# Second block: attention outputs with tokens on partitions, head norms on eight columns, no division of probabilities

## What is computed

```
p = jax.nn.softmax(s, axis=-1)                      # heads 0 to 7
oa, ob = moba_attention(...), dsa_attention(...)    # p @ v per head
z = einsum(q, k) * scale                            # heads 8 to 15
a = exp(log_sigmoid(z) + reverse_cumsum(log_sigmoid(-z), strictly after))
oc = a @ v
o = concatenate([oa, ob, oc])                       # (tokens, 16 heads, 64)
o = o * rsqrt(mean(o * o, over the 64) + 1e-6) * out_g
x = x + g2 * (o @ w_out)
```

## Time and profile before

| | |
|---|---|
| median of 3 runs | 2840.96 us |
| the profiled execution | 2840.38 us, of which its span is 2838.3 us |
| mean granted TensorE clock | 0.994 |
| PE, DVE, ACT, POOL busy | 98%, 70%, 48%, 8% |
| attention passes, layer 0 of the second block | from about 2008.6 us to 2063.2 us of the span |
| the same, second layer | from about 2566 us to 2621 us of the span |

### The profile page before, as it was taken

One profiled execution on the slowest core, in us unless ns is written; L12 is line 12 of the kernel. 1 busy time (PEld: TensorE's weight loads), 2 busy tenths in 40 slices (PEclk: granted clock), 3 DMA queues, 4 the chain that ended last, 5 costly groups with the idle time before them and its releaser, 6 DMA issues.

```text
span 2838.3 us, 37704 instructions
## 1 busy us (share of the span) xinstructions
PE 2773.7 (98%) x16040; PEld 2423.6 (85%) x16040; DVE 1974.6 (70%) x2225; ACT 1370.5 (48%) x1554; POOL 228.9 (8%) x201
## 2 busy tenths in 40 slices
PE   7999999999999999999999999999999999999999
PEld 6889999998888889999998887878878878787787
DVE  6768876655666678877655667677976676778644
ACT  5444545455444445545454444444644444446433
POOL 0000420000000000520000000003000000030000
PEclk9999999999999999999999999999999999999999
DMA  8655433445776655333446666653266666442453
GB/s 304 258 220 183 151 122 137 165 164 211 260 262 246 251 207 188 139 135 133 171 165 229 256 256 245 258 217 134 90 229 253 252 264 259 182 149 95 177 188 149
DMA packets 82039, 564.43 MB, mean 199 GB/s; under 512 B 9072, under 2 KB 10576, under 8 KB 15952
## 3 DMA queue, kind: packets, MB, share of 16 engines
q1 hardware_dynamic: 66272, 465.47, 44.9%
q0 software_dynamic: 15600, 96.55, 9.1%
HBM read 560.86 MB, written 1.12 MB: 198 GB/s over the span
## 4 chain that ended last, share of the span: by engine, by line
PE 82%; DVE 11%; ACT 3%; POOL 2%; DMA 1%; issue 1%; SPq 0%; POOLq 0%; ACTq 0%; DVEq 0%
PE ps L332 74%; DVE ring_lo L327 3%; ACT w_hi L320 1%; POOL qk L2038 1%; PE ps L899 1%; POOL rope_a L2034 1%; DVE a_hg L1806 1%; DMA rows<-mod_rows 1%; DVE e L1786 1%; DVE e L1785 1%; PE ps L1287 1%; DVE h_lo L576 0%; PE ps L1416 0%; PE ps L1442 0%; DVE e L993 0%
## 5 line engine op out<-in xcount | busy, mean ns | idle before, releaser
L327 DVE TENSOR_TENSOR ring_lo<-ring,w_hi 128x2048 fp32r<-128x2048 f32 x422 | 973.8, 2310 | 478.9 <-ACT w_hi L320 467.3
L320 ACT ACTIVATE w_hi<-ring 128x2048 fp32r<-128x2048 f32 x422 | 806.4, 1911 | 321.5 <-PE ps L332 197.9
L332 PE MATMUL ps<-w_hi,h_hi 128*128 128x512 f32 (+1 forms) x1920 | 729.1, 380 | 18.0 <-DVE ring_lo L327 9.3
L332 PE MATMUL ps<-w_hi,h_lo 128*128 128x512 f32 (+1 forms) x1920 | 716.4, 373 | 0.0
L332 PE MATMUL ps<-ring_lo,h_hi 128*128 128x512 f32 (+1 forms) x1920 | 716.0, 373 | 0.0
L332 PEld LDWEIGHTS ps<-w_hi,h_hi 128*128 128x128 f32 x1920 | 363.1, 189 | 86.3 <-DVE ring_lo L327 11.9
L332 PE MATMUL ps<-h_hi,w_hi 128*128 128x256 f32 x1488 | 430.8, 290 | 1.3 <-DVE h_lo L576 1.3
L332 PE MATMUL ps<-h_lo,w_hi 128*128 128x256 f32 x1488 | 422.3, 284 | 0.0
L332 PE MATMUL ps<-h_hi,ring_lo 128*128 128x256 f32 x1488 | 422.3, 284 | 0.0
L332 PEld LDWEIGHTS ps<-w_hi,h_lo 128*128 128x128 f32 x1920 | 362.9, 189 | 64.6
L332 PEld LDWEIGHTS ps<-ring_lo,h_hi 128*128 128x128 f32 x1920 | 363.6, 189 | 61.4 <-issue 1.6
(11 more groups left out here) (356 smaller groups left out, 3446.0 us busy)
## 6 DMA issues: line engine op xcount, KB each, us to landing
ring<-stream SPq DMA_DIRECT2D x438, 1024.0 KB, 4.8
e<-ada POOLq DMA_DIRECT2D x77, 1024.0 KB, 5.9
rows<-mod_rows POOLq DMA_DIRECT2D x18, 512.0 KB, 5.9
rows<-gain_rows POOLq DMA_DIRECT2D x8, 512.0 KB, 4.4
val<-c_row POOLq DMA_DIRECT2D x4, 512.0 KB, 5.5
x<-x_in SPq DMA_DIRECT2D x4, 256.0 KB, 7.2
mem<-mem_t SPq DMA_DIRECT2D x1, 1024.0 KB, 16.4
out_t<-x SPq DMA_DIRECT2D x4, 256.0 KB, 2.1
```

Source lines behind the costliest of these rows:

```text
L320: nc.scalar.activation(hi_of(p), ring[:, p % RING, :], ACT.Copy).then_inc(S.w_hi_ready, 1)
L327: nc.vector.tensor_tensor(lo_of(p), ring[:, p % RING, :], hi_of(p).bitcast(F32), ALU.subtract).then_inc(S.w_lo_ready, 1)
L332: mm = nc.tensor.matmul(out, a, b, start=start and n == 0, stop=stop and n == 2, skip_group_check=group)
```

## The change

Scores, sticks, masks and sums stay as they are. What changes, for each of the two layers:

- `normalise` is gone: `flip` waits for `exp_ready`. The sums of the exponentials, which `exps` gets with its accumulating output, go to `exp_sum` (32 columns, preset to 1.0 for the stick heads by a memset).
- `weigh` has the probabilities as its stationary side (128*128) and 64 columns of values as its moving side: three matmuls for a head in place of two. Outputs have tokens on partitions. The four pairs use PSUM banks 7, 3, 7 and 4 (`OUT_BANK`).
- A head norm is now one number per token and head: eight columns for a pair. ACT squares (`pair_sq`), DVE sums 64 columns at a time and adds the scaled epsilon (`pair_stat`), ACT does Ln and Exp on eight columns, DVE refines them and multiplies the bank by them into `o_tok` (`pair_scaled`).
- PE turns the result back by four transposes into the same bank (`turn_back`), ACT rounds it with the gain as its scale (`pair_high`), and DVE makes the rest from PSUM (`pair_low`), which signals `o_ready`.
- PE's `turn_back(3)` stands behind the first 24 products of the out projection. ACT and DVE have the new steps inside their loops; DVE's `pair_scaled` stands ahead of `stick_arg` of the same pass.

```diff
+        OUT_BANK = (7, 3, 7, 4)
+        o_tok = hk[:].rearrange("p k t -> p (k t)").rearrange("p (j n) -> p j n", j=4)
...
             def flip(n):
-                pe.wait_ge(S.probs_ready, nth(S.probs_ready, n + 1))
+                pe.wait_ge(S.exp_ready, nth(S.exp_ready, n + 1))
...
+            def weigh(n, kind, head, w, ready, done):
+                j = n // 2
                 pe.wait_ge(ready, nth(ready, n + 1))
+                if j == 1:
+                    pe.wait_ge(S.evac_done, nth(S.evac_done, 15))
+                elif j == 2:
+                    pe.wait_ge(S.o_ready, nth(S.o_ready, 1))
+                elif j == 3:
+                    pe.wait_ge(S.scores_read, nth(S.scores_read, HEADS_2 - 1))
+                v = (kind * HEADS_2 + head) * HD
+                at = kind * P + (head % 2) * HD
+                to = ps[:, OUT_BANK[j], :]
+                nc.tensor.matmul(to[:, at:at + HD], w[:, 0:P], val[:, 0, v:v + HD], start=True, stop=True, ...)
+                nc.tensor.matmul(to[:, T + at:T + at + HD], w[:, P:T], val[:, 0, v:v + HD], start=True, stop=False, ...)
+                nc.tensor.matmul(to[:, T + at:T + at + HD], w[:, T:3 * P], val[:, 1, v:v + HD], start=False, stop=True, ...)
...
+            def turn_back(j):
+                pe.wait_ge(S.o_scaled, nth(S.o_scaled, j + 1))
+                for kind in range(2):
+                    for t in range(2):
+                        at = t * T + kind * P
+                        mm = nc.tensor.transpose(ps[:, OUT_BANK[j], kind * T + t * P:kind * T + (t + 1) * P],
+                                                 o_tok[:, j, at:at + P], ident)
+                mm.then_inc(S.o_turned, 1)
...
-            for i in range(HEADS_2 + 3):
+            for i in range(HEADS_2 + 2):
...
-                if i >= 4 and i % 2 == 0:
-                    pair_sums((i - 4) // 2)
+                if i >= 5 and i % 2 == 1:
+                    turn_back((i - 5) // 2)
...
+            pe.wait_ge(S.o_ready, nth(S.o_ready, 2))
             for c in range(2):
...
                 mm.then_inc(S.tile_done, 1)
+                if c == 0:
+                    turn_back(3)
...
-            def pair_out(j):
+            def pair_sq(j):
...
+                nc.scalar.activation(e_buf[0][...512 columns...], ps[:, OUT_BANK[j], :], ACT.Square).then_inc(S.o_sq, 1)
             def pair_rstd(j):
...
+                chain(nc.scalar.activation(o_rs[:, j, :], o_ms[:, j, :], ACT.Ln))
+                nc.scalar.activation(o_rs[:, j, :], o_rs[:, j, :], ACT.Exp, scale=-0.5).then_inc(S.o_rstd, 1)
+            def pair_high(j):
+                act.wait_ge(S.o_turned, nth(S.o_turned, j + 1))
+                for kind in range(2):
+                    k = 4 * kind + j
+                    ins = nc.scalar.activation(h_hi[:, k, :], ps[:, OUT_BANK[j], kind * T:(kind + 1) * T], ACT.Copy,
+                                               scale=v_now[:, V2_OUT + k:V2_OUT + k + 1])
+                ins.then_inc(S.o_hi_ready, 1)
             for i in range(HEADS_2 + 4):
+                if 0 <= i - 2 < HEADS_2 and i != 3:
+                    flipped(i - 2)
+                if i >= 5 and i % 2 == 1:
+                    pair_rstd((i - 5) // 2)
+                if i < HEADS_2:
+                    exps(i)
...
                 if i >= 4 and i % 2 == 0:
-                    pair_out((i - 4) // 2)
-                if i < HEADS_2:
+                    pair_sq((i - 4) // 2)
+                if i >= 5 and i % 2 == 1:
+                    pair_high((i - 5) // 2)
+                if i < HEADS_2 and i != 3:
                     softplus(i)
...
+            def pair_stat(j):
+                dve.wait_ge(S.o_sq, nth(S.o_sq, j + 1))
+                nc.vector.tensor_reduce(o_ms[:, j, :], e_buf[0][...8 heads x 64...], AX.X, ALU.add)
+                chain(nc.vector.scalar_tensor_tensor(out=o_eps[:, j, :], in0=exp_sum[:, j, :], scalar=EPS,
+                                                     in1=exp_sum[:, j, :], op0=ALU.mult, op1=ALU.mult))
+                nc.vector.scalar_tensor_tensor(out=o_ms[:, j, :], in0=o_ms[:, j, :], scalar=1.0 / HD,
+                                               in1=o_eps[:, j, :], op0=ALU.mult,
+                                               op1=ALU.add).then_inc(S.o_var, 1)
             def pair_scaled(j):
                 dve.wait_ge(S.o_rstd, nth(S.o_rstd, j + 1))
+                refine(chain, o_rs[:, j, :], o_ms[:, j, :])
+                nc.vector.tensor_tensor(o_tok[...], ps[:, OUT_BANK[j], :]..., o_rs[:, j, :]...broadcast_to([P, 8, HD]),
+                                        ALU.mult).then_inc(S.o_scaled, 1)
+            def pair_low(j):
+                dve.wait_ge(S.o_hi_ready, nth(S.o_hi_ready, j + 1))
+                for kind in range(2):
+                    k = 4 * kind + j
+                    ins = nc.vector.scalar_tensor_tensor(out=h_lo[:, k, :],
+                                                         in0=ps[:, OUT_BANK[j], kind * T:(kind + 1) * T],
+                                                         scalar=v_now[:, V2_OUT + k:V2_OUT + k + 1],
+                                                         in1=h_hi[:, k, :].bitcast(F32), op0=ALU.mult,
+                                                         op1=ALU.subtract)
+                ins.then_inc(S.o_ready, 1)
+            chain(nc.vector.memset(stat[:, 0:32], 1.0))
+            for i in range(HEADS_2 + 4):
...
+                if i >= 5 and i % 2 == 1:
+                    pair_scaled((i - 5) // 2)
                 if 0 <= i - 2 < HEADS_2:
                     stick_arg(i - 2)
                 if 0 <= i - 1 < HEADS_2:
-                    normalise(i - 1)
                     stick_log(i - 1)
...
+                if i >= 4 and i % 2 == 0:
+                    pair_stat((i - 4) // 2)
                 if i >= 5 and i % 2 == 1:
-                    pair_var((i - 5) // 2)
-                if i >= 6 and i % 2 == 0:
-                    pair_scaled((i - 6) // 2)
+                    pair_low((i - 5) // 2)
```

More of the change, by code:

```diff
@@ L2322, in sums @@
                                  skip_group_check=True).then_inc(S.cum_done, 1)
-            def weigh(n, w, v, at, ready, done):
+            def weigh(n, kind, head, w, ready, done):
+                j = n // 2
                 pe.wait_ge(ready, nth(ready, n + 1))
-                if n >= 2:
-                    pe.wait_ge(S.o_sq, nth(S.o_sq, n // 2))
-                r = slice(HD * (n % 2), HD * (n % 2 + 1))
-                nc.tensor.matmul(ps[r, 7, at:at + T], val[:, 0, v:v + HD], w[:, 0:T], start=True, stop=False,
+                if j == 1:
[7 more added lines that the diff above has]
+                to = ps[:, OUT_BANK[j], :]
+                nc.tensor.matmul(to[:, at:at + HD], w[:, 0:P], val[:, 0, v:v + HD], start=True, stop=True,
@@ L2701, in pair_scaled @@
             def pair_scaled(j):
                 dve.wait_ge(S.o_rstd, nth(S.o_rstd, j + 1))
-                vv, rr = (e[:, 2 * j:2 * j + 2, :] for e in (e_buf[1], e_buf[0]))
-                refine(chain, rr, vv)
-                for b in range(2):
-                    k = 4 * b + j
-                    ins = nc.vector.scalar_tensor_tensor(out=hk[:, k, :], in0=hk[:, k, :],
-                                                         scalar=v_now[:, V2_OUT + k:V2_OUT + k + 1],
-                                                         in1=rr[:, b, :], op0=ALU.mult, op1=ALU.mult)
```

77 lines of the change are left out of this document (24 added, 53 removed).

## The result

The changed kernel takes 2844.28 us (median of 20 runs, 2837.73 to 2848.46), the kernel before in the same session 2840.15 us (20 runs, 2837.61 to 2843.03). The ratio is 1.0013 with a 95% interval of 1.0007 to 1.0019: slower by some 4 us. The forecast was 1.4 us faster, 2839.6; the time lies inside the range of 2835.2 to 2844.5 and above the forecast's own of 2836.5 to 2843, and the change went the other way.

The account below looks back on a forecast made before the run. PE was taken to set the pace, held up by DVE and ACT in both attention stretches. The walk gave 51.9 us against 52.6, for two layers 1.4 less: 2839.0, for the median 2839.6, range 2835.2 to 2844.5.

Parts of the forecast that it names:

- the clock's 1.7: Attention stretch with out projection, kernel before: 1.7 us a layer above the 52.6 walk, put down to PE's clock, left unchanged.
- The durations: Prices of single steps on PE, ACT and DVE, issue to issue, taken from profile rows, most with bounds.
- the two waits: In a head's weighing, a wait for each of two halves, raising twelve records from 1.38 to 1.52 us.
- the first rival: Weighing goes by columns: 0.84 us a head, 6.4 us less in all, 2834.5; chance 0.10.
- The walk at full pace: Layer 0 from its second flip through the out projection, step by step: 51.9 us against 52.6 before, 0.7 less.
- The places of the idle times: PE's four idles on the walk in layer 0: 1.1, 2.5, 1.5 and 0.9 us, longest ahead of head 6's sums.
- DVE's waits in `pair_low`: DVE idle about 1 us ahead of the first `pair_low` and 2.5 ahead of the second.
- One sign of being wrong: PE idling less than 4 us in all would show the forecast wrong, with the kernel then faster.
- The third rival: PE's clock stays low from pair 1's transposes to the 24th product: 13 us in all, 2854; chance 0.05.
- a window after one long idle: Argument against the slow clock: after a 2.82 us idle the window shows 0.69, the loss ending after some 4 us.
- The second rival: Round trip between weighing and rest longer than the rows say: at upper bounds 5.2 us more, 2846.1; chance 0.11.
- a walk at half pace to the 24th product: Layer walk with PE's 1.2 GHz work taking twice its time: 60.8 us against 54.26, 13 us in all.

Follow-up runs that it names:

- the second comparison: The changed kernel run again without an edit, against the kernel before: mean 2844.06 against 2841.18 us, ratio 1.0010.
- e_after_fill: Changed kernel plus 17 matmuls a layer that nobody reads, in three of PE's waits: 2839.60 us, 0.9991 against the kernel before.
- e_fill_one: Changed kernel plus nine matmuls that nobody reads, only ahead of the sums of head 6: 2841.09 us, 1.0001 against the kernel before.
- e_order: Changed kernel with `pair_scaled` behind `stick_log`, `pair_low` one pass later and softplus ahead of `pair_high`: 2834.68 us, 0.9975 against the kernel before.
- e_order_fill: Changed kernel with those three steps moved, plus 11 matmuls that nobody reads in PE's remaining waits: 2833.47 us, 0.9974 against the kernel before.
- The filled runs: Kernels with matmuls that nobody reads in PE's waits; on the changed kernel, all three waits filled took 2839.60 us, one filled 2841.09.

## Why the prediction was wrong

The step that failed is the sentence "PE is idle in it four times, [...] about as much as before in all, so I leave the clock's 1.7 as they are". The idle time in all was indeed no more than before (3.92 us in layer 0 and 5.08 in the second, against 4.54 and 5.26). But the clock didn't follow the sum. Time at 1.2 GHz was 7.2, 3.6, 3.6 and 3.6 us in the four profiled stretches of before, and 10.4, 10.4, 24.0 and 10.4 in those of the changed kernel. Counted from the stretches with the clock up (58.86 and 57.04), that cost 0.7 us a layer before, where I had put 1.7 down to the clock, and 3.3 after, where I left the same 1.7. With 1.8 less at full clock this is 0.8 more a layer, 1.5 in all. Measured were 4.1 (medians of 20 runs) and 2.9 (means of the second comparison). That the loss is the clock's is shown by e_after_fill; how it divides is not: the two profiled executions of the changed kernel are 5.0 us longer on average than those of before, of which 1.5 lie in the stretches, 2.2 ahead of the first and 1.4 between the two, in code that is all but the same.

Point by point:
- The durations held. Weighing 1.38 where I took 1.52 (the two waits cost nothing), so the first rival (0.84, by columns) fell; transposes of a pair 0.44 for 0.45; sums of squares with their two small steps 0.88 for 0.96 (2039.17 - 2038.29); scaling 1.20 for 1.29; inverse root 0.35 for 0.36; rounding 0.73 for 0.85 (2058.31 - 2057.58); rest 0.80 for 0.89 (2059.25 - 2058.45). All are issue to issue, all a little under my value.
- The walk at full pace was on the right side and too long: with the clock up a layer is 1.8 us shorter than before, where I had 0.7. In the second layer of e_fill_one the out projection starts 33.8 us after the second flip, where the walk has 35.1.
- The places of the idle times: the longest was ahead of the sums of head 6, as forecast, at 2.10 for 2.5; the others 0.81 and 0.56 (1.72 in the second layer) for 1.1, 1.5 and 0.9. DVE's waits in `pair_low` were 0.76 for 1, and 3.89 for 2.5; the excess of the second is PE at half pace, whose sums and transposes it waits for. In the second layer, where the clock was still up, it is 2.54:
```profile
2613.96 0.87 DVE L2730 SCALAR_TENSOR_TENSOR h_lo<-ps,v_now,h_hi 128x256 fp32r<-128x256 f32 x2 [2.54 <-ACT h_hi L2517]
```
- The out projection started 35.7 us after the second flip, forecast 35.1, the transposes of pair 3 ready inside it. That is luck: a walk 1.3 too long and a clock that I had left out of it nearly cancel. So is the time inside the range.
- One sign of being wrong pointed the wrong way: PE idled less than 4 us in layer 0 (3.92), and the kernel was slower, not faster.
- The third rival, the slow clock, had the right mechanism and a chance of 0.05. It said that it decides from a loss of 5.2 us a layer on, and the stretches lost 3.3 on average; its price of 13 us in all was too high, because the clock came back after 10.4 us in three of the four stretches, ahead of or early in the out projection, and because part of the slow work fell into PE's waits. I had argued against it with a window after one long idle. A window behind one idle time didn't tell what four in a row do, and the row was of another order of waits.
- The second rival, a longer round trip, fell: every handing over was in reach of its rows.

What stays open is why the same program falls for 10.4 us in one layer and 24 in another, with the same waits, and whether some of the difference outside the stretches is due to the change. With two executions of either kernel profiled, chance is enough to explain it: e_order and e_order_fill, the same first block, have none and two of the spells near 380 and 1200 us. The filled runs bound it: they bring the mean clock back to 0.9927, by edits in the stretches alone.

## What to carry to other kernels

An engine's idle time has a price of its own beside its length: when a change puts several shorter waits of PE where one stood, the sum of the waits doesn't give what the clock will cost. Take the low clock as a likely case and not as the tail, and size it from stretches of the same program with the clock up and down: here 10.4 us at 1.2 GHz cost 1.8 to 3.5 us, and a walk at half pace to the 24th product gave 13 us for the 4 that were measured. A loop of three engines in order is best checked by asking, at each wait, what stands behind it that another engine needs; moving three steps behind such work took the kernel from 2.9 us over before to 7.0 under it (means), about half of it by the order itself (4.7 us by the stretches with the clock up). A suspected loss to the clock is tested in one run, by filling the idle time with matmuls that nobody reads.
